# Two layers of gated convolution and pooling on one core: all six roles of token half 0 first, and squares summed by TensorE

## The reference, cut to what matters

```python
for l in range(2):
    shift, scale, gate = split(silu(c) @ w_ada[l] + b_ada[l], 3)
    h = rms_norm(x, g_pre[l]) * (1 + scale) + shift
    u_a, b_a, c_a, gate_a, u_p, gate_p = split(h @ w_in[l], 6)       # 512 columns each
    y_a = b_a * causal_depthwise_conv(c_a * u_a, w_conv[l]) * silu(gate_a)
    y_p = causal_multiscale_pool(u_p, w_pool[l], pool_scale[l]) * silu(gate_p)
    y = concat(y_a, y_p) @ w_out[l]
    x = x + gate * rms_norm(y, g_post[l])
out = hybrid_layer(x, ...)                                           # not touched
```

## Time and profile before

| | |
|---|---|
| median of 3 runs | 2295.85 us |
| the profiled execution | 2294.0 us |
| its span, first to last instruction | 2292.2 us |
| mean granted TensorE clock | 0.956 |
| PE busy | 2168.5 us, 95% |
| DVE, ACT, POOL busy | 1093.6, 752.1, 225.6 us |

### The profile page before, as it was taken

One profiled execution on the slowest core, in us unless ns is written; L12 is line 12 of the kernel. 1 busy time (PEld: TensorE's weight loads), 2 busy tenths in 40 slices (PEclk: granted clock), 3 DMA queues, 4 the chain that ended last, 5 costly groups with the idle time before them and its releaser, 6 DMA issues.

```text
span 2292.2 us, 26136 instructions
## 1 busy us (share of the span) xinstructions
PE 2168.5 (95%) x9910; PEld 1737.5 (76%) x9910; DVE 1093.6 (48%) x1702; ACT 752.1 (33%) x1191; POOL 225.6 (10%) x194
## 2 busy tenths in 40 slices
PE   6999999799999989999988898999999999999987
PEld 5888888678888777578865667868788888888876
DVE  6553454553332463776778874473312222222244
ACT  2311114432111442655766554242111112111134
POOL 1000002410000231021210000320000000000032
PEclk6899999879999999999979999999999999999997
DMA  7343333211111332111110002221211111121122
GB/s 288 95 123 105 101 102 90 66 47 55 46 55 46 115 97 68 47 30 28 51 33 1 1 1 100 88 70 51 60 46 43 49 55 46 41 60 46 39 76 87
DMA packets 223483, 151.60 MB, mean 66 GB/s; under 512 B 6549, under 2 KB 211494, under 8 KB 223270
## 3 DMA queue, kind: packets, MB, share of 16 engines
q1 hardware_dynamic: 217824, 133.48, 19.2%
q0 software_dynamic: 4608, 16.78, 2.3%
q10 hardware_dynamic: 966, 0.21, 0.0%
HBM read 142.06 MB, written 8.39 MB: 66 GB/s over the span
## 4 chain that ended last, share of the span: by engine, by line
PE 81%; DVE 8%; ACT 5%; issue 2%; POOL 2%; DMA 1%; ACTq 0%; DVEq 0%; SPq 0%; POOLq 0%
PE pair L1916 47%; PE pair L1932 16%; PE pair L2088 4%; PE pair L2056 3%; PE pair L2189 2%; PE pair L2157 2%; PE pair L1900 1%; DVE act_region L1596 1%; PE pair L2171 1%; PE pair L2076 1%; DVE w_lo L1241 1%; POOL sum L692 1%; ACT proj L934 1%; PE pair L1881 1%; ACT w_hi L740 1%
## 5 line engine op out<-in xcount | busy, mean ns | idle before, releaser
L1247 DVE TENSOR_TENSOR w_lo<-w_raw,w_hi 128x1024 fp32r<-128x1024 f32 x101 | 123.8, 1226 | 687.0 <-ACT w_hi L747 687.0
L1916 PE MATMUL pair<-act_hi,w_hi 128*128 128x512 f32 x1328 | 409.5, 390 | 3.9 <-ACT v_all L875 1.8
L1916 PE MATMUL pair<-act_lo,w_hi 128*128 128x512 f32 x1328 | 408.9, 389 | 0.0
L1916 PE MATMUL pair<-act_hi,w_lo 128*128 128x512 f32 x1328 | 408.9, 389 | 0.0
L747 ACT ACTIVATE w_hi<-w_raw 128x1024 fp32r<-128x1024 f32 x102 | 108.2, 1061 | 824.8 <-PE pair L1916 824.8
L1916 PEld LDWEIGHTS pair<-act_hi,w_hi 128*128 128x128 f32 x1328 | 248.6, 188 | 58.2 <-issue 4.9
L1916 PEld LDWEIGHTS pair<-act_hi,w_lo 128*128 128x128 f32 x1328 | 249.3, 188 | 51.9
L1916 PEld LDWEIGHTS pair<-act_lo,w_hi 128*128 128x128 f32 x1328 | 249.2, 188 | 51.8
L1932 PE MATMUL pair<-act_hi,w_hi 128*128 128x512 f32 x576 | 238.9, 415 | 21.6 <-DVE w_lo L1241 7.2
L1241 DVE TENSOR_TENSOR w_lo<-w_raw,w_hi 128x1024 fp32r<-128x1024 f32 x92 | 121.6, 1322 | 240.4 <-ACT w_hi L740 240.2
L1932 PE MATMUL pair<-act_lo,w_hi 128*128 128x512 f32 x576 | 232.2, 403 | 0.0
(11 more groups left out here) (338 smaller groups left out, 3116.1 us busy)
## 6 DMA issues: line engine op xcount, KB each, us to landing
w_raw<-w_in SPq DMA_DIRECT2D x72, 512.0 KB, 3.8
w_raw<-w_out SPq DMA_DIRECT2D x48, 512.0 KB, 3.9
w_raw<-w_gu SPq DMA_DIRECT2D x48, 512.0 KB, 3.8
w_raw<-w_down SPq DMA_DIRECT2D x32, 384.0 KB, 3.1
act_region<-w_ada SPq DMA_DIRECT2D x16, 512.0 KB, 14.1
sq<-w_ada POOLq DMA_DIRECT2D x16, 512.0 KB, 4.3
sq_sum<-w_ada POOLq DMA_DIRECT2D x16, 512.0 KB, 4.8
yT<-x SPq DMA_DIRECT2D x8, 512.0 KB, 7.2
```

Of the source, the lines that this page charges most:

```text
L1247: v.tensor_tensor(w_lo[s_][:], w_raw[s_][:], f32(w_hi[s_][:]), ALU.subtract)\
L1916: i = mm(bank[pair][:, h * HALF:(h + 1) * HALF], w[slot][:, k, :], a[:, k, h * HALF:(h + 1) * HALF], start=(k == 0 and w is w_hi and a is ...
```

## The change

Turn 0 of both layers now has 6 half products for half 0 and then 6 for half 1, and roles 4 and 5 have no full product. Role 4's and 5's half 0 is written to the second half of PSUM pairs 0 and 1. ACT copies them out at once (`p_first`, `gp_first`) and signals `p_half` and `gp_half`, for which PE waits ahead of the half products of half 1 that overwrite these places. So a layer has 28 input units instead of 26. DVE and ACT do the roles as before behind the half products of half 1.

The squares of x go to eight buffers, halves of `u_buf`, `conv`, `gate_buf` and `cu`, which are free then. PE takes all of them by 128x1 matmuls: for half 0 four after product d = 3 and four after d = 4, and POOL's `x_sum` is gone; for half 1 two after role 2, four after role 3 and two in the middle of role 4, with the spread in the middle of role 5. In layer 1 DVE's difference for the first weight of half 1 stands behind chunk 4's scaling.

```diff
-P1_LOOP = P1_ROLES + SPLIT
-P1_UNITS = P1_ROLES * CB + SPLIT
+P1_LOOP = 2 * P1_ROLES
+P1_UNITS = P1_ROLES * CB + P1_ROLES
...
+        def x_square(k):
+            return (u_buf, conv, gate_buf, cu[:, TAPS - 1:])[k // 2][:, half(k % 2)]
...  SP
-                    load_in(l, l * UL + q, q % 2, 0, q % SPLIT if q < 2 * SPLIT else q - SPLIT)
+                    load_in(l, l * UL + q, q % 2, 0, q % P1_ROLES)
...  POOL: x_sum and its calls removed
-                if l == 0:
-                    x_sum(range(4))
-                y_sum(l, 1, range(3, 4))
-                if l == 0:
-                    x_sum(range(4, KT))
-                y_sum(l, 1, range(4, KT - 1))
+                y_sum(l, 1, range(3, KT - 1))
...  ACT
                     x_updated(0, a, k)
-                    if k >= 2:
-                        act.wait_ge(sq_taken if a else xsq_added, k - 1)
-                    A(sqs[k % 2][:, half(a)], xT[:, k, half(a)], ACT.Square).then_inc(xsq_ready, 1)
+                    A(x_square(k), xT[:, k, half(a)], ACT.Square).then_inc(xsq_ready, 1)
...  ACT, role 4 and 5 of turn 0
+                    if split:
+                        A(p_buf[:, PAD + HALF:], bank[0][:, half(1)], ACT.Copy).then_inc(p_copied, 1)
...
+                    if split:
+                        act.wait_ge(gp_half, 2 * l + 1)
+                        A(gp_buf[:, half(0)], gp_buf[:, half(0)], ACT.Silu).then_inc(gp_half, 1)
+                        A(gp_buf[:, half(1)], bank[1][:, half(1)], ACT.Silu).then_inc(gp_done, 1)
...
+            def p_first(l):
+                act.wait_ge(unit_done, 2 + l * UL + 5)
+                act.wait_ge(pooled, 1 + CB * l)
+                A(p_buf[:, PAD:PAD + HALF], bank[0][:, half(1)], ACT.Copy).then_inc(p_half, 1)
+
+            def gp_first(l):
+                act.wait_ge(unit_done, 2 + l * UL + 6)
+                act.wait_ge(y_pool, 1 + CB * l)
+                A(gp_buf[:, half(0)], bank[1][:, half(1)], ACT.Copy).then_inc(gp_half, 1)
...  ACT, turn 0
-                for q in range(SPLIT):
+                for q in range(P1_ROLES):
                     hi_at(base + q + 2)
+                    if q == 4:
+                        p_first(l)
+                    if q == 5:
+                        gp_first(l)
...
                     if l and q == 3:
                         root(4, 1)
-                        in_hi(1, 1, range(KT))
+                    if l and q == 4:
+                        in_hi(1, 1, range(5))
+                    if l and q == 5:
+                        in_hi(1, 1, range(5, KT))
...  DVE, turn 0 of layer 1
+                    lo_at(base + 4)
+                    lo_at(base + 5)
+                    rooted(4, 1)
+                    in_scale(1, 1, range(2))
+                    for k in range(2, KT):
+                        in_lo(1, 1, range(k - 2, k - 1))
+                        in_scale(1, 1, range(k, k + 1))
+                        if k == 4:
+                            lo_at(base + 6)
+                    in_lo(1, 1, range(KT - 2, KT))
+                    lo_at(base + 7)
...
                 for r in range(P1_ROLES):
-                    lo_at(base + SPLIT + r + 2)
+                    lo_at(base + P1_ROLES + r + 2)
                     role(l, 0, r)
...  PE
+            def x_stat(a, ks):
                 for k in ks:
+                    pe.wait_ge(xsq_ready, a * KT + k + 1)
+                    for t in range(TT // 2):
+                        i = mm(bank[3][:, a * HALF + t:a * HALF + t + 1], x_square(k)[:, t * P:(t + 1) * P], ones[:, 0:1],
+                               start=k == 0 and t == 0, stop=k == KT - 1 and t == TT // 2 - 1)
                 if k == KT - 1:
+                    i.then_inc(stat_done, 1)
...
+                for q in range(P1_ROLES):
+                    if q == 2 and l:
                         pe.wait_ge(t_ready, 3 * KT)
+                    chain_step = None
+                    if l and q == 1:
+                        chain_step = lambda: spread(1, 5)
+                    if l and q == 4:
+                        chain_step = lambda: x_stat(1, range(6, KT))
+                    if l and q == 5:
+                        chain_step = lambda: spread(1, 6)
+                    half_product(base + q, q % SPLIT, q // SPLIT, (lambda k: split_at(4 * l * KT, k)) if q == 0 else None,
+                                 between=chain_step, tokens=0)
+                    if l and q == 0:
+                        y_stat(0, 1, 3)
+                    if l and q == 2:
+                        x_stat(1, range(2))
+                    if l and q == 3:
+                        x_stat(1, range(2, 6))
+                for q in range(P1_ROLES):
                     if q == 0:
+                        pe.wait_ge(p_half, l + 1)
+                    if q == 1:
+                        pe.wait_ge(gp_half, 2 * l + 1)
+                    if q == 4:
+                        pe.wait_ge(u_copied, CB * l + 1)
+                    if q == 5:
+                        pe.wait_ge(c_used, 1 + CB * l + 1)
+                    half_product(base + P1_ROLES + q, q % SPLIT, 1,
+                                 (lambda k: split_at((4 * l + 1) * KT, k)) if q == 0 else None)
+                pool_mix(l, 0)
...  PE, layer 0's output of half 1
-                    if l == 0 and d == 4:
-                        pe.wait_ge(xsq_added, KT)
-                        token_cols(sq_sum, bank[3], 0, True, True).then_inc(stat_done, 1)
+                    if l == 0 and d in (3, 4):
+                        x_stat(0, range(4 * (d - 3), 4 * (d - 2)))
```

More of the change, by code:

```diff
@@ L625, in x_odds @@
                     g.tensor_tensor(xT[:, k, half(a)], xT[:, k, half(a)], yT[:, k, half(a)], ALU.add).then_inc(x_odd, 1)
[L627 to L636, removed]
             for l in range(LAYERS):
@@ L793, in o_taken, with role @@
                 A(yT[:, d, half(a)], o, ACT.Copy).then_inc(o_copied, 1)
-            def role(l, j, r):
+            def role(l, j, r, split=False):
                 n = CB * l + j
@@ L835, in _ @@
                 for r in range(P1_ROLES):
-                    hi_at(base + SPLIT + r + 2)
-                    role(l, 0, r)
+                    hi_at(base + P1_ROLES + r + 2)
+                    role(l, 0, r, split=True)
                 with loop(act, CB - 1) as j:
@@ L1352, in _ @@
                 base, out0 = l * UL, l * UL + P1_UNITS
-                for q in range(SPLIT):
-                    if l == 0:
+                if l == 0:
+                    for q in range(P1_ROLES):
                         lo_at(base + q + 2)
@@ L1357, in _ @@
                             in_lo(0, 1, range(4 * q, 4 * q + 4))
[L1358 to L1374, removed]
+                else:
+                    lo_at(base + 2)
+                    rooted(3, 1)
+                    y_normed(0, 1, range(4))
+                    lo_at(base + 3)
+                    y_normed(0, 1, range(4, KT))
+                    lo_at(base + 4)
[9 more added lines that the diff above has]
+                    lo_at(base + 7)
                 dve.wait_ge(s_lo, (4 * l + 2) * KT)
                 for r in range(P1_ROLES):
-                    lo_at(base + SPLIT + r + 2)
+                    lo_at(base + P1_ROLES + r + 2)
                     role(l, 0, r)
@@ L1919, in product, with half_product @@
                 i.then_inc(unit_done, 1)
-            def half_product(u, b, a, wait_split=None, order=range(KT), hi=act_hi, lo=act_lo, between=None):
+            def half_product(u, b, a, wait_split=None, order=range(KT), hi=act_hi, lo=act_lo, between=None, tokens=None):
                 pe.wait_ge(hi_ready, 1 + u + 2)
@@ L1925, in half_product @@
                 o = bank[b][:, half(a)]
+                tokens = half(a if tokens is None else tokens)
                 for k in order:
@@ L1931, in half_product @@
                     for w, x_ in ((w_hi, hi), (w_hi, lo), (w_lo, hi)):
-                        i_ = mm(o, w[u % 2][:, k, :], x_[:, k, half(a)], start=(k == order[0] and w is w_hi and x_ is hi),
+                        i_ = mm(o, w[u % 2][:, k, :], x_[:, k, tokens], start=(k == order[0] and w is w_hi and x_ is hi),
                                 stop=(k == order[-1] and w is w_lo))
@@ L1946, in pooling, with pool_mix @@
                 product(u + 1, 1, 1)
+                pool_mix(l, j)
+            def pool_mix(l, j):
+                n = CB * l + j
                 pe.wait_ge(pooled, 1 + n + 1)
@@ L1987, in x_stat_late @@
                 if k == KT - 1:
-                    pe.wait_ge(sq_taken, KT)
-                    pe.sem_inc(stat_done, 1)
+                    i.then_inc(stat_done, 1)
             for l in range(LAYERS):
                 base, out0 = l * UL, l * UL + P1_UNITS
[L1993 to L1997, removed]
-                        pe.wait_ge(t_ready, 3 * KT)
-                    half_product(base + q, q, 0, (lambda k: split_at(4 * KT, k)) if q == 0 else None,
```

(7 more changed lines are left out.)

17 lines of the change are left out of this document (6 added, 11 removed).

## The result

The changed kernel took 2300.76 us (median of 14 runs, 2297.44 to 2309.01) against 2295.73 us of the kernel before (14 runs, 2294.12 to 2297.32). The ratio is 1.0026 with an interval of 1.0017 to 1.0034: 5.0 us slower, where 6.9 had been forecast. Measured once more beside the last experiments it took 2298.19 us against 2295.27, a ratio of 1.0018 (1.0008 to 1.0029).

A forecast was written before the change was run, and what follows sets the result against it. PE, busy for 95% of the span, was taken as the bound. Terms of +11.5, -3.8 and -0.8 us summed to +6.9, stated as 2302.7 us, with a range of 2293.5 to 2310.5.

The forecast's parts named there:

- term 1: Layer 0's first turn: the mix starts 8.3 us later behind DVE, plus 3.2 for the clock; +11.5 us.
- term 2: Layer 0's output, token half 1: PE's 11.3 us wait for POOL goes, groups of four cost clock; -3.8 us.
- term 3: Layer 1's first turn: old waits go, PE idles for the first half 1 weight and the mix; -0.8 us.
- my upper end: Layer 0's first turn with the clock's loss at its most: 14.9 us.
- the clock's share: Loss to PE's slower clock behind idling or small matmuls; at layer 0's mix 0 to 6.6 us, 3.2 taken.
- The rival in which DVE is covered after all: Layer 0's first turn: late pieces and windows no longer hold the mix; -4.6 us, 2291.2; chance 0.12.
- The rival of a clock that spares the gaps: Both layers: new gaps and groups of four cost no clock; -7.9 us, 2288; chance 0.13.
- the lottery: PE's clock: a free-running activity window makes each clock charge random, so one kernel measures differently by its phase at start.

The follow-up runs named there:

- experiment 3: The changed kernel with layer 1's first turn in the old order, layer 0 and the squares as changed; 2302.18 us, 1.0031 against the kernel before.
- experiment 9: The changed kernel unaltered, measured and profiled again; 2298.19 us, the profiled execution with a span of 2293.7 us.
- experiment 4: The changed kernel with DVE summing layer 0's eight late pieces during roles 2 to 5 of half 0; 2297.89 us, 1.0011 against the kernel before.
- experiment 6: Experiment 4 plus window operations run over each token half by itself in both layers' first turns; 2287.94 us, 0.9958 against the kernel before.
- experiment 7: The kernel before with only half 0's squares changed, their 128x1 groups in twos instead of fours, spread behind product 5; 2285.10 us, 0.9957.
- experiment 5: The changed kernel with DVE's difference for layer 1's first half 1 weight ahead of the first scaling; 2300.11 us, 1.0015 against the kernel before.
- experiment 8: The changed kernel with late pieces early, windows by halves, layer 1's weight difference early and groups of two in both halves; 2277.93 us, 0.9921.
- experiment 2: The changed kernel with layer 0's first turn in the old order, layer 1 and the squares as changed; 2290.38 us, 0.9980 against the kernel before.

## Why the prediction was right

The mechanism was, and the sum nearly so. By the medians, term 1 is 11.1 us (11.5 forecast), term 2 -4.1 (-3.8) and term 3 -0.7 (-0.8); by experiment 3, term 3 would be -2.0 or -4.1 instead. That single terms came within half a microsecond is luck, with intervals of 2 us and more and with the clock's share in each of them. Their sum, 6.3, is 1.3 and 3.4 us above the two measurements of the changed kernel; over a spread of 12 to 14 us between its runs I don't read anything into that.

Term 1: the mix came at 142.20 in the first profile (141.7 forecast), and DVE's stretch, from the end of role 1's second half to the last window operation, was 111.17 to 142.16 = 31.0 us (30.3), the difference being a longer wait for one late piece, 2.48 against 1.86 us. In the other profile (experiment 9) that wait was 1.58 us and the stretch 29.7. The first profile's two gaps were 2.22 and 4.80 us and not 1.8 and 6.7, because the first one already brought the clock down and lengthened the product between. In the other profile the first gap was 1.03 us, the clock held, and the second was 6.20. The start of the first looped product plus its slow beginning gives 14.9 us, my upper end; in the other profile it was 10.7, below the middle, and 1.0 of that had arisen before the end of role 1's second half (112.12 against 111.17). So the size of the clock's share, 0 to 6.6, was right as a range and is no fixed number.

What the term's account lacked is how much of it had a second cause waiting. I credited the late pieces with all of it when I designed experiment 4, though my own term 3 held the row that said otherwise: in layer 1, without any pieces, the mix waits 3.6 us. In layer 0, 3.6 us belong to the window operations and some 5 to the pieces. The rival in which DVE is covered after all needed both to go, and experiment 6 is that rival made true, in both layers: 12.8 us faster than the first measurement of the changed kernel, 10.3 than the second.

Term 2: the 11.3 us wait went without a successor, ACT's squares and the cast for product 5 were early as forecast, and both sets of four brought the clock to 1.2 GHz in the first profile (7.10 for a product of 5.44, then 5.33 for 12 matmuls against 2.72). In the other profile only the second did (5.62, then 5.33). The 2.2 us charged for each were right in size: by experiment 7, in which only their spacing and the place of one spread differ, the two cost 4.7 us together by the rows and 6.0 by the medians. The rest of the term holds as well: without a clock loss it was to be -8.2 us, and experiment 7, which has none there, is 8.1 us shorter than before over that stretch (103.06 against 111.15).

Term 3: the gap for the first weight was 4.22 us (4.2 forecast) and the one at the mix 3.60 (3.6). The agreement on the first is part luck, since 6.75 - 2.72 is 4.0 and not 4.2; the sum behind it also ends at 544.7 and not 544.9. The half product behind the gap took 8.2 us (517.39 to 525.62), where 8.5 had been taken. What the term didn't see is what lies behind the first gap: it is not worth its length, since DVE's 1.32 us for each chunk hold the same half product anyhow (experiment 5).

The rival of a clock that spares the gaps was no full case, but the lottery beside it is there: the runs of the changed kernel lie 11.6 and 14.1 us apart, those of the kernel before 3.2 and 3.0, and the five of experiment 8, in which the gaps treated here are all under 1 us, 2.2. It isn't the length of a gap that does it, for the kernel before has its 11.3 us wait, and the wait of over 7 us outside the changed stages stands in the profiles of all three. Nor is it any gap of 2 to 5 us: experiment 2, with layer 1's gaps of 4.21 and 3.60 us, spreads over 4.4 us in 11 runs, experiment 3, with layer 0's pair, over 6.1 in 9, and kernels with such gaps in both layers over 11.5 and more (experiments 4, 5 and 9). Why the spread grows so is open.

The Trainium skill (TensorE: Matmul & The Clock Gate, Part 1, "What's actually happening") says that the window is free-running and the cost differs by its phase. The two profiles of one program agree with that: an idle time of 1.8 us ahead of layer 0's first output product cost PE its clock in one (52.10 us) and not in the other (49.22), and behind layer 0's mix the same three microseconds stand at 0.50 and at 1.00. That it is the phase that decides is the page's word; no run here set it.

## What to carry to other kernels

When a stage is split so that more of it goes ahead, what is left behind gets shorter too; count the slowest engine's work from its last release to the next join, and compare it with the products that still stand there. Here that was 31 us against 21.8, and it put the mix 8.8 us later where PE had not waited before (142.20 against 133.39), while layer 1's stalls gave back less than one by the medians.

Put matmuls of few columns in small lots between full ones: the same eight groups cost 6.0 us less by the medians in twos than in fours, 4.7 by the rows. And look at the spread first: where the runs of one kernel lie 12 us apart, as here with several PE gaps of 2 to 6 us, time ten or more before believing a difference of 3 us.

## What the runs showed that I had not expected

An idle time of PE can cost more than its length. Taking out 5.7 us of gaps gained 10.0 us (experiment 6), and the second gap of a pair is shorter for the clock that the first has taken. It needn't: breaking up the gap of 4.22 us (experiment 5) showed nothing in the median. And two executions of one program, no instruction different, lay 11.5 us apart, with 4.2 us of that standing at the end of the first loop turn behind one wait (217.11 against 212.90).
